# Moving the split feed-forward weights by 16 bytes inside their SBUF buffers

## The reference

```python
def swiglu(x, wg, wu, wd):
    return (jax.nn.silu(x @ wg) * (x @ wu)) @ wd      # wg, wu: 1024 x 2816; wd: 2816 x 1024

for l in range(DEPTH):                                # DEPTH = 2
    h = swiglu(rmsnorm(x, ffn1_pre_g[l]), ffn1_wg[l], ffn1_wu[l], ffn1_wd[l])
    x = x + 0.5 * rmsnorm(h, ffn1_post_g[l])
    m, new = token_mix(rmsnorm(x, mix_pre_g[l]), l, ...)   # RWKV-7, RG-LRU and HGRN2 branches, gated merge
    x = x + rmsnorm(m, mix_post_g[l])
    h = swiglu(rmsnorm(x, ffn2_pre_g[l]), ffn2_wg[l], ffn2_wu[l], ffn2_wd[l])
    x = x + 0.5 * rmsnorm(h, ffn2_post_g[l])
```

## The kernel before

| operand | start | modulo 256 |
|---|---|---|
| `uh`, `ul` (gate, up and mixer input; each tile 1280 further) | 47520, 57760 | 160, 160 |
| `hfh`, `hfl` (down input; each tile 1280 further) | 138016, 166176 | 32, 32 |
| `whi0`, `whi1` (pieces 512 apart) | 194336, 202528 | 32, 32 |
| `wlo0`, `wlo1` | 104544, 112736 | 96, 96 |
| rooms H0 (in `whi0`) and SS | 194336, 123552 | 32, 160 |
| rooms P0 and P3 | 168736, 181024 | 32, 32 |

## Time and profile before

### The profile page before, as it was taken

The page is one execution under the profiler, slowest core; times in us unless marked ns, Lnnn a source line. Parts: engine busy times, 40 slices in busy tenths (PEclk is TensorE's granted clock), DMA queues, the critical chain, the costliest instruction groups (busy, mean ns, idle before and its releaser), DMA issues.

```text
span 2037.9 us, 36447 instructions
## 1 busy us (share of the span) xinstructions
PE 1990.9 (98%) x15192; PEld 1779.0 (87%) x15192; DVE 1304.6 (64%) x1997; ACT 779.2 (38%) x932; POOL 84.5 (4%) x164
## 2 busy tenths in 40 slices
PE   7999999999999999999999999999999999999998
PEld 6999988777677798999999999987776778999998
DVE  5776387666467676655377755866665676676644
ACT  4444363322332344333344444623324223443332
POOL 1111000000000000000011100000000000000000
PEclk9999999999999999999999999999999999999999
DMA  6888533343323343444458874333443334434442
GB/s 242 306 299 281 185 110 111 116 128 124 136 107 118 134 166 104 144 144 165 165 191 309 300 245 154 132 109 116 137 136 116 115 114 149 145 106 150 156 159 95
DMA packets 60844, 327.03 MB, mean 160 GB/s; under 512 B 7249, under 2 KB 7441, under 8 KB 34481
## 3 DMA queue, kind: packets, MB, share of 16 engines
q1 hardware_dynamic: 43200, 262.99, 37.5%
q0 software_dynamic: 17520, 62.27, 8.6%
HBM read 290.87 MB, written 34.36 MB: 160 GB/s over the span
## 4 chain that ended last, share of the span: by engine, by line
PE 92%; DVE 4%; ACT 1%; DVEq 1%; DMA 1%; issue 1%; SPq 0%
PE dps L702 45%; PE dps L606 11%; PE dps L556 10%; PE mx L756 9%; PE dps L641 8%; PE mx L923 1%; PE mx L658 1%; PE dps L629 1%; DMA raw<-in_wstream 1%; PE mx L939 1%; PE mx L976 1%; PE mx L953 1%; DVE tmp L1791 1%; DVE rs L1483 1%; PE mx L556 1%; DVE ho L1425 1%
## 5 line engine op out<-in xcount | busy, mean ns | idle before, releaser
L1053 ACT ACTIVATE whi<-raw 128x2048 fp32r<-128x2048 f32 (+1 forms) x144 | 269.2, 1869 | 487.3 <-PE dps L702 470.3
L702 PE MATMUL dps<-uh,whi 128*128 128x320 f32 x1408 | 430.2, 306 | 19.8 <-DVE wlo L1422 15.1
L1422 DVE TENSOR_TENSOR wlo<-raw,whi 128x2048 fp32r<-128x2048 f32 x136 | 311.7, 2292 | 209.0 <-ACT whi L1053 203.9
L702 PE MATMUL dps<-uh,wlo 128*128 128x320 f32 x1408 | 434.3, 308 | 0.0
L702 PE MATMUL dps<-ul,whi 128*128 128x320 f32 x1408 | 433.0, 307 | 0.0
L702 PEld LDWEIGHTS dps<-uh,whi 128*128 128x128 f32 x1408 | 264.8, 188 | 25.2 <-issue 18.5
L702 PEld LDWEIGHTS dps<-uh,wlo 128*128 128x128 f32 x1408 | 264.9, 188 | 0.0
L702 PEld LDWEIGHTS dps<-ul,whi 128*128 128x128 f32 x1408 | 264.0, 187 | 0.6
L606 PE MATMUL dps<-u,raw 128*128 128x320 f32 x768 | 235.7, 444 | 0.0
L702 PE MATMUL dps<-hfh,whi 128*128 128x320 f32 x704 | 220.4, 313 | 0.0
L702 PE MATMUL dps<-hfh,wlo 128*128 128x320 f32 x704 | 217.6, 309 | 0.0
(11 more groups left out here) (295 smaller groups left out, 3191.0 us busy)
## 6 DMA issues: line engine op xcount, KB each, us to landing
raw<-in_wstream SPq DMA_DIRECT2D x198, 1024.0 KB, 4.8
u<-in_wstream POOLq DMA_DIRECT2D x44, 512.0 KB, 7.0
split_store<-wha POOLq DMA_DIRECT2D x44, 512.0 KB, 7.5
raw<-in_wstream SPq DMA_DIRECT2D x44, 512.0 KB, 4.1
parts<-split_store SPq DMA_DIRECT2D x44, 512.0 KB, 5.2
hs<-in_st_hgrn POOLq DMA_DIRECT2D x8, 512.0 KB, 5.7
out_o_hgrn<-hs POOLq DMA_DIRECT2D x8, 512.0 KB, 2.9
out_yT<-x SPq DMA_DIRECT2D x2, 1280.0 KB, 4.5
```

The source lines that it names most:

```text
L702: m = pe.matmul(dps[:, 2 * half + c, 0:T], w[:, k, c * P:(c + 1) * P], v[:, k0 + k, :], start=first and k == 0 and i == 0, stop=last and k ...
L1053: return nc.scalar.activation(out, in_, f, **kw)
L1422: return nc.vector.tensor_tensor(out, a, b, op)
```

## The change

The four views of the split weights become four words longer, and what the kernel calls `whi[s]` and `wlo[s]` starts at their fifth word. All uses (the split, the products, the rooms H0 and H1) follow. No instruction is added or taken away.

```diff
-        tmp, *wlo = shared("tmp", 13 * T, views=[("wlo0", (BLK,)), ("wlo1", (BLK,))])
+        tmp, *wlo = shared("tmp", 13 * T, views=[("wlo0", (BLK + 4,)), ("wlo1", (BLK + 4,))])
+        wlo = [w[:, 4:4 + BLK] for w in wlo]
...
-        ov, hfh, hfl, *whi, ovr = shared("ov", 64, T, views=[("hfh", (KF, T)), ("hfl", (KF, T)), ("whi0", (BLK,)), ("whi1", (BLK,))],
-                                         whole=[("ovr", (64, T))])
+        ov, hfh, hfl, *whi, ovr = shared("ov", 64, T, views=[("hfh", (KF, T)), ("hfl", (KF, T)), ("whi0", (BLK + 4,)),
+                                                             ("whi1", (BLK + 4,))], whole=[("ovr", (64, T))])
+        whi = [w[:, 4:4 + BLK] for w in whi]
```

## The result

The changed kernel takes 2056.23 us (median of 4 runs, 2056.03 to 2056.47) against 2039.6 for the kernel before (median of 4 runs); the ratio is 1.0085, 95% interval 1.0073 to 1.0098, so 15 to 20 us slower. The profiled execution has a span of 2054.6 us, 16.7 more than before.

What follows compares the result with a forecast made beforehand. TensorE's pitch of matmul starts was taken to bound the kernel; all terms were taken as 0, summing to 0 on a span of 2037.9 us, with the forecast made at the runs' median, 2039 us; 8-in-10 range 2014 to 2060.

Steps and rivals of the forecast that it cites:

- What bounds the kernel: Whole kernel: TensorE, in flight for 98% of the span; the pitch of matmul starts sets the end.
- The splits: 136 block copies on ScalarE and 136 subtractions on VectorE: the offset start costs 0 for both engines.
- The mixer's rooms: 144 half-block mixer matmuls using the room in whi0: under 1 us even at 6.7 ns each, taken as 0.
- The deciding term: 6336 matmuls of L702 loading weights from the moved buffers: bounded between -59 and +42 us, taken as 0.
- gate and up lose their fast pace: Gate and up products: 1408 triples go from 433.3 to 440 ns, +9.4 us, 2048.6; chance 0.19.
- no change: Whole kernel: time stays within 2035 to 2043, the spread of the runs; chance 0.36.
- A step on every matmul: L702: a load starting mid 32 bytes needs one more piece, delaying each matmul, +42 us, 2081; chance 0.11.
- one step better: Down gets the fast pace and gate and up gain one more step: -14 us, 2025; chance 0.22.
- Reads no longer meet: L702 products: all excess over streaming but 2.5 ns a matmul goes, -59 us, 1980; chance 0.12.

Runs made afterwards that it cites:

- e3: Kernel before with both weight buffers, both slots, moved by 32 bytes: 2051.99 us, ratio 1.0074.
- e4: Kernel before with both weight buffers, both slots, moved by 256 bytes: 2038.64 us, ratio 1.0002.
- e5: e3 with the inputs uh and ul also moved by 32 bytes, restoring gate and up's relation but not down's: 2040.24 us, ratio 1.0011.
- e9: TensorE alone, without the kernel's computation: selected places repeated, single tiles, other widths, plain fp32; five repeated places took 433 to 447 ns a triple at 320 columns.
- e7: Kernel before with only the high weights moved, by 16 bytes in both slots: 2045.97 us, ratio 1.0039.
- e1: TensorE alone at the kernel before's addresses; cells (high, low) move the weights 0 to 15 lines of 16 bytes; median 440.0 ns a triple.
- e6: Kernel before with hfh and hfl 128 bytes and high weights 256 bytes further, giving down gate and up's relation: 2033.07 us against 2038.99.

## Why the prediction was wrong

**What bounds the kernel** held: no wait is new, the splits took the same time, and the whole difference is the pace of L702's matmuls, closed to within 1 us.

**The splits** at nothing were right: 1918 and 2293 ns, and VectorE's slack before TensorE only grew (1.32 us against 1.15). **The mixer's rooms** at nothing could not be told apart; 144 matmuls are too few.

**The deciding term was wrong.** The prediction had shown that place matters and then took 0 for an unknown place, since "the rows nearest in size to a move of 16 or 48 bytes are that of 64 bytes in `wlo`". That nearness was empty: the table has no smoothness from one line to the next. From (0, 0) = 434 all four next lines in rows and columns that were tried, (0, 1), (1, 0), (0, 15), (15, 0), are 438.5 or more. What the rows did say was that gate and up stood at the fastest pace of any family of triples in the kernel while most others stood at 440. For a start from the best cell, any move is like a draw from all cells, and their median turned out to be 440. The step that failed is this one, and with it the ranking: the rival "gate and up lose their fast pace", with 0.19, was the mechanism, and was shown by e3, e4 and e5.

**Its size was off as well**: +9.4 us expected of it, +15.6 measured. The prediction read "the steps are single: 6.7 ns a triple or none" from the few families at hand; e9 has steady paces of 442 to 447 and the new places are 443.7 and 445.6. The time, 2056, lies between that rival's 2049 and the other's 2081, inside the range of 2014 to 2060; that is owed to the width of the range, since the forecast had no change and leaned, 0.34 to 0.30, to faster.

**"A step on every matmul"** from the middle of 32 bytes is not what happened: multiples of 32 are as slow (e3), and one odd line can be fast (e7 in down). For the weights, the Trainium skill's 16-byte cachelines (page "SBUF — State Buffer", section "SBUF: two separate sides") agree with this: weights at 16 modulo 32 have no price of their own, a mean of 440.2 against 440.1. For the inputs an odd line does have one, 441.3 to 441.8 against 433.3 to 433.5 for even lines once settled (e1). The Trainium skill's statement that a weight load takes no read bandwidth from the running matmul (page "TensorE: Matmul & The Clock Gate", section "Step-by-step: what each phase is for") fits plain fp32 in these runs, 269.2 ns at the four places tried. It does not account for fp32r, where moving the weights against the inputs changes the pace by up to 3%; that read bandwidth is what is lost there is not shown either.

**The two faster rivals**: "one step better" is real for down (e6, -4.6 us by the paces) and not for gate and up, which no cell of the table brings below 433.3. "Reads no longer meet" was seen nowhere: the lowest pace of any cell of 320 columns is 432.3 ns, with inputs one line and weights five lines further (e9).

**What stays open** is the mechanism behind the table. Shown is that the pace hangs on the place of the weights relative to the inputs (443.3 in e3, 433.4 in e5, with the weights in the same relation to each other) and that no other engine need be at work (e1). That the reading of the weights and that of the inputs get in each other's way is the likely reason, but it is an inference: which resource they would share, why 256 bytes is the period, and why one place can settle at two paces are not shown. Whether a finer step than 16 bytes matters was tried at five points of e1 only: both weights moved by 4, 8, 12, 20 or 24 bytes gave 443.3, 440.0, 441.0, 444.5 and 436.7 ns.

## What to carry to other kernels

Where TensorE is the bound and works in fp32r, the place of the weights against the moving tile, modulo 256 bytes, sets some 3% of the pace, and it can't be reasoned from neighbouring places: measure a table of places with the kernel's own shapes and order, then put the buffers into a good cell. Give each cell more than eight triples, leave out the first ones, and run it after different cells, as one place can settle at two paces. A good cell is confirmed in the whole kernel only. Before moving a buffer, look whether its matmuls already run at the best pace that the kernel shows anywhere; if they do, a move can only lose, and the slower products are those to move. A "nearest row" bounds a cost only if the quantity is known to vary smoothly; if the rows show it jumping, treat an untried place as a draw from all places.

## What the runs showed of the hardware that was not expected

- Triples of fp32r matmuls of 320 columns take 433.3 to 448.5 ns by place in e1, against 400 of streaming. Plain fp32 takes 269.2 ns an instruction at each of the four places tried.
- The dependence has a period of 256 bytes (e1, e4) and is reproducible to 0.2 ns a triple (e9, each cell after the same cell), in a kernel of matmuls alone; the pace of the whole kernel is within 1.1 ns of the table's in the pairs compared above, the slots of the changed kernel included, but for gate and up of e5 (433.4 against 435.3, with the slower first triples in it).
- One place can settle at two paces, depending on what ran before: cell (0, 4) at 440 ns in e1 and at 433.3 in e9. A cell can take three triples to settle (e1).
- Inputs that start on an odd line of 16 bytes have other paces than inputs on an even line in the same relation: 441.3 to 441.8 against 435.3 to 435.7, or 433.3 to 433.5 once settled (e1).
- The best place depends on the width: (0, 0) is the best of four places at 320 columns and the worst of them at 256.
